# Writing out every engine loop of a decoder step, with all semaphore waits on constants

## The reference

```python
def layer(x, l, mem_k, mem_v, shift_prev, wkv_prev, conv_prev, ffn_prev, v_first, P):
    xn = rmsnorm(x, P['norm_mix'][l])
    proj = xn @ w_in                                   # 1024 -> 3328
    y_a, wkv_new, v_first = rwkv7_group(p_rwkv, p_prev, wkv_prev, v_first, l, P)
    conv_out, conv_new = causal_dwconv(gate_c * h_in, conv_prev, P['conv_w'][l])
    x = x + jnp.concatenate([y_a, gate_b * conv_out], axis=-1) @ P['w_out'][l]
    q = rmsnorm(x, P['norm_x'][l]) @ P['wq'][l]        # 4 heads x 256, 256 memory tokens
    x = x + softmax_attention(q, mem_k, mem_v) @ P['wo'][l]
    up = rmsnorm(x, P['norm_ffn'][l]) @ P['w_up'][l]   # 1024 -> 2 x 2816
    upc, ffn_new = causal_dwconv(up, ffn_prev, P['ffn_conv_w'][l])
    u, gt = jnp.split(upc, 2, axis=-1)
    x = x + (jax.nn.silu(gt) * u) @ P['w_down'][l]
```

## Time and profile before

| | |
|---|---|
| time, median of 3 runs | 4897.39 us |
| the three runs | 4886.02, 4897.39, 4908.73 us |
| span of the profiled execution, first to last instruction | 4900.2 us |
| TensorE busy | 4308.0 us, 88% of the span |
| VectorE, ScalarE, GpSimd busy | 2273.0, 1456.1, 1416.4 us |
| mean granted TensorE clock | 0.914 of full speed |
| moved by DMA | 320.54 MB, 65 GB/s |

### The profile page before, as it was taken

The page is one execution under the profiler, slowest core; times in us unless marked ns, Lnnn a source line. Parts: engine busy times, 40 slices in busy tenths (PEclk is TensorE's granted clock), DMA queues, the critical chain, the costliest instruction groups (busy, mean ns, idle before and its releaser), DMA issues.

```text
span 4900.2 us, 72602 instructions
## 1 busy us (share of the span) xinstructions
PE 4308.0 (88%) x22425; PEld 3583.0 (73%) x22425; DVE 2273.0 (46%) x4969; ACT 1456.1 (30%) x2858; POOL 1416.4 (29%) x1222
## 2 busy tenths in 40 slices
PE   3789988998889989997989889997989787899996
PEld 3569866886679757885779667885879665678885
DVE  1246534545255535454266535444154553245554
ACT  1333233333333233333323233333322212022222
POOL 6232032443231123442331124442221011023331
PEclk9899998998889999998999899997998888699997
DMA  2320122332310112332310213332210112222221
GB/s 73 125 69 1 43 69 65 94 94 73 103 44 1 60 52 86 94 97 77 88 32 0 78 44 103 94 94 78 64 31 0 52 35 86 90 61 73 68 68 57
DMA packets 454929, 320.54 MB, mean 65 GB/s; under 512 B 18012, under 2 KB 420262, under 8 KB 453070
## 3 DMA queue, kind: packets, MB, share of 16 engines
q1 hardware_dynamic: 454758, 318.45, 21.1%
HBM read 296.99 MB, written 21.61 MB: 65 GB/s over the span
## 4 chain that ended last, share of the span: by engine, by line
PE 68%; DVE 15%; issue 9%; POOL 3%; ACT 3%; DMA 1%; DVEq 1%; ACTq 0%; POOLq 0%; SPq 0%
PE psum L671 66%; DVE xlo L1429 2%; PE psum L675 2%; POOL wlo L577 1%; DVE xT L1429 1%; DVE shifted L1429 1%; DVE zr L1432 1%; DVE ws L1429 1%; ACT whi L1102 1%; DVE shifted L1432 1%; DVE kkn_y L1429 1%; POOL stage L519 1%; DVE xT L1432 0%; DMA out_y_prompt<-zr 0%; ACT stage L1102 0%
## 5 line engine op out<-in xcount | busy, mean ns | idle before, releaser
L577 POOL TENSOR_TENSOR wlo<-wraw,whi 128x1024 fp32r<-128x1024 f32 x480 | 1152.3, 2401 | 2818.6 <-ACT whi L1102 2818.5
L671 PE MATMUL psum<-xhi,whi 128*128 128x512 f32 (+1 forms) x3136 | 1254.3, 400 | 58.5 <-DVE xlo L1429 41.1
L671 PE MATMUL psum<-xhi,wlo 128*128 128x512 f32 (+1 forms) x3136 | 1224.0, 390 | 0.0
L671 PE MATMUL psum<-xlo,whi 128*128 128x512 f32 (+1 forms) x3136 | 1224.0, 390 | 0.0
L1102 ACT ACTIVATE whi<-wraw 128x1024 fp32r<-128x1024 f32 x480 | 507.4, 1057 | 1226.2 <-PE psum L671 1161.4
L671 PEld LDWEIGHTS psum<-xhi,whi 128*128 128x128 f32 x3136 | 599.7, 191 | 231.6 <-DVE xlo L1429 81.1
L671 PEld LDWEIGHTS psum<-xhi,wlo 128*128 128x128 f32 x3136 | 599.7, 191 | 125.0
L671 PEld LDWEIGHTS psum<-xlo,whi 128*128 128x128 f32 x3136 | 601.2, 192 | 113.0 <-issue 1.4
L1429 DVE TENSOR_TENSOR xT<-xT,psum 128x512 f32<-128x512 f32 (+1 forms) x416 | 286.0, 688 | 246.0 <-PE psum L671 166.5
L1741 DVE TENSOR_SCALAR zr<-zr,fcw 128x512 f32<-128x512 f32 x176 | 91.9, 522 | 585.2 <-POOL fcarry L619 583.5
L671 PE MATMUL psum<-ws 128*128 128x64 f32 (+1 forms) x2560 | 350.7, 283 | 2.1 <-DVE ws L1595 1.7
(11 more groups left out here) (292 smaller groups left out, 5587.7 us busy)
## 6 DMA issues: line engine op xcount, KB each, us to landing
wraw<-in_w_up SPq DMA_DIRECT2D x176, 512.0 KB, 3.8
wraw<-in_w_in SPq DMA_DIRECT2D x104, 512.0 KB, 3.9
wraw<-in_w_down SPq DMA_DIRECT2D x88, 512.0 KB, 3.5
wraw<-in_w_out SPq DMA_DIRECT2D x32, 512.0 KB, 4.1
wraw<-in_wq SPq DMA_DIRECT2D x32, 512.0 KB, 4.0
wraw<-in_wo SPq DMA_DIRECT2D x32, 512.0 KB, 4.1
kkn_y<-in_x_prompt SPq DMA_DIRECT2D x4, 2048.0 KB, 9.3
xT_scratch<-xT SPq DMA_DIRECT2D x4, 2048.0 KB, 7.6
```

What stands on the lines that cost most here:

```text
L577: return e.tensor_tensor(wlo[i][:, :, :], wraw[i][:, :, :], whi[i][:, :, :].bitcast(F32), ALU.subtract).then_inc(lo_ready[i], 1)
L671: return e.matmul(out, lhsT, rhs, start=start, stop=stop)
```

## The change

All hardware loops become loops of the program that writes the instructions, so each turn's instructions stand in the stream one after the other. Turn numbers are then constants, and so is every wait's value and every address. The register operations, the branches and the three `passed` semaphores go. The order of the work on data, the buffers and the other semaphores stay. The diff, cut to its core; the same edit is made at each loop and at each count of `passed`:

```diff
 class Counts:
-    def __init__(self, eng, name, passed=None):
-        self.eng, self.name, self.passed, self.n, self.turns = eng, name, passed, {}, []
+    def __init__(self):
+        self.n = {}

     def __call__(self, sem, k=1):

         v = self.n[sem.name] = self.n.get(sem.name, 0) + k
-        for i, per in self.turns:
-            if per.get(sem.name):
-                v = i * per[sem.name] + v
         return v
...
-    @contextmanager
-    def loop(self, label, count):
-        key = f"{self.name}.{label}"
-        per, before = LOOPS.get(key, {}), dict(self.n)
-        if self.passed is not None and self.turns:
-            self.eng.sem_inc(self.passed, 1)
-        with self.eng.Fori(0, count) as i:
...
             def carries(a, tile):
                 e.wait_ge(eb_ready[a], c(eb_ready[a]))
-                e.sem_inc(passedG, 1)
...
-                with c.loop("ffn", NF // 2 - 1) as i:
+                for i in range(NF // 2 - 1):
                     ffn_up(i + 1)
                     ffn_down(i)
...
-            with c.loop("block", NB - 1) as b:
+            for b in range(NB - 1):
                 one_block(b, False)
             one_block(NB - 1, True)
```

More of the change, by code:

```diff
@@ L580, in splits @@
             def splits(label, pairs):
-                with c.loop(label, pairs):
+                for _ in range(pairs):
                     split(0)
@@ L937, in one_block @@
                 head_rows(8)
-                with c.loop("gates" + "s" * last, 4):
+                for _ in range(4):
                     dense(0, 0, s)
@@ L944, in one_block @@
                 wkv_pair(True)
-                with c.loop("wkv", NC // 2 - 1):
+                for _ in range(NC // 2 - 1):
                     wkv_pair()
@@ L986, in one_block @@
                 ffn_up(s, tuple(range(KT)))
-                with c.loop("ffn" + "s" * last, NF // 2 - 1):
+                for _ in range(NF // 2 - 1):
                     ffn_up(s)
@@ L1138, in _ @@
                 split_x(k, NMEM)
[L1139 removed]
+            for _ in range(8):
                 for j in range(2):
@@ L1352, in one_block @@
                 ffn_hidden()
-                with c.loop("ffn" + "s" * last, NF // 2 - 1) as i:
+                for i in range(NF // 2 - 1):
                     ffn_up(i + 1)
@@ L1644, in residual @@
                 acc_start()
-                with c.loop(label + "s" * last, KT // 2) as i:
+                for i in range(KT // 2):
                     for j in range(2):
@@ L1884, in one_block @@
                 e.wait_ge(a2v, c(a2v, 4))
-                with c.loop("h_in" + "s" * last, 2) as i:
+                for i in range(2):
                     for j in range(2):
```

158 lines of the change are left out of this document (22 added, 136 removed).

## The result

| | before | after |
|---|---|---|
| median of four runs | 4900.91 us | 4784.85 us |
| lowest and highest | 4886.02, 4908.73 us | 4781.53, 4790.23 us |

The ratio is 0.9764, with a 95% interval of 0.9744 to 0.9783. Six more runs of the changed kernel, with another set of runs of before, gave 4781.80 us and 0.9739 (0.9713 to 0.9764).

The account below looks back on a forecast made before the run. TensorE, busy 88% of the time, was taken as the bound, with register operations costing where short dependent chains reach it late. Terms of 8.9 + 10.5 + 8 + 6.4 + 7.5 + 0.5 = 42 us gave 4855 us, range 4812 to 4890.

Parts of the forecast that it names:

- A: Back-edges of the block loop: both crossings that branch back become as short as the one falling through, 8.9 us.
- the carry-to-silu chain: Convolution chain in `ffn` of blocks 0 to 2: from 2.90 us to the constant form's 2.55 us.
- C: `ffn` turns of the last block: two TensorE gaps per turn that end on VectorE's sequencer shrink, 8 us.
- the supply of instructions: Rival, slower by fetching straight code: some 270 packets, up to 5118 us if each fully blocked TensorE; chance 0.08.
- B: `ffn` turns of blocks 0 to 2: 0.35 us of register operations saved in each of 30 turns, 10.5 us.
- the cap of 0.39: Most that a shorter chain could give at an `ffn` turn's edge: 0.39 us per turn, 11.8 us in all.
- the fall-through: Crossing into the last block without branching back, 32.81 us, taken as the form of all three crossings after the change.
- D: `wkv` pairs: removing both levels of turn numbers gains 6.4 us; upper bound 19 us, all of TensorE's idle time.
- the nearest row: `wkv` pair with one level of turn numbers less: 51.44 to 51.26 us, 0.18 us, taken twice for the second level.
- The counts of `passed`: Extra semaphore counts on which nobody waits: their removal was put at nothing.
- E: Norms, attention and projections' edges: 2.5 us a block, 7.5 us for blocks 0 to 2; bounds 0 and 49 us.
- The clock: Low-clock stretch in one last-block `wkv` pair, 22.8 us: 23 us either way, in the range but not the sum.

Follow-up runs that it names:

- dve_wkv_kept: Changed kernel, but VectorE's loop over chunk pairs in `wkv` stays a hardware loop with one level of turn numbers: 4825.23 us.
- dve_clean: Kernel before, with all loops written out on VectorE alone and VectorE's extra counts taken out too: 4821.03 us.
- passed_kept: Changed kernel, straight code with constant waits, but the extra counts of `passed` stay behind their waits: 4806.98 us.
- dve_only: Kernel before, with all loops written out on VectorE alone and the extra counts left in: 4813.20 us.
- blk_only: Kernel before, with only the block loop written out, on all engines; shorter loops stay hardware loops: 4857.03 us.
- gap_d: Changed kernel with 18 small fills in each `wkv` pair on VectorE, behind waits for TensorE, without register operations: 4810.00 us.
- late_a: Changed kernel with 40 small fills of an unused tile on VectorE ahead of the first block: 4790.73 us.

## Why the prediction was wrong

**What held.** The signs and places of the parts that it named; the 5.6 us ahead of block 0 were in none. TensorE was the bound, A's back-edges went, the carry-to-silu chain fell to 2.55 us, the gaps of C closed, and the supply of instructions cost nothing: packets rose to 179 (270 were estimated), while TensorE ran 2320 matmuls in 426.05 us without a break. In B the eight middle turns of a block gave 0.44 us each, 10.4 us in all. That is above the cap of 0.39, whose pace of 0.229 us had counted in the length of the turn's last matmul. The other 7.5 us of B lie in the first turn and after the ninth, at the edges of the stage, which the sum had left out. A was 3 us short, since the fall-through, its model, got faster as well (32.81 to 32.17 us) and the other two fell below it.

**The step that failed first: D.** The prediction took "the nearest row", 0.18 us for one level of turn numbers, and doubled it for the other level. The levels are not alike: a middle pair takes 51.45 us with two, 51.17 with one (dve_wkv_kept), 49.99 with none. The second level costs 0.28 us; the first costs 1.2 us, together with the loop's end and VectorE's counts, which go with it. The upper bound, TensorE's idle time in the pair (1.6 us, 19 us in all), was the better estimate: 18.3 us were had. That is partly luck, since half of the idle time is left and TensorE's busy time fell instead.

**The edit costed at nothing: the counts.** "The counts of `passed`, on which nobody waits" looked at who waits for them, not at where they stand. Each is an instruction of its own between a wait and the data behind it. Left in, they cost 22 us in the finished kernel, of which the profile books 9 us directly and the rest in attention's clock. Whose counts are the costly ones is open: taking VectorE's out beside engines with loops (dve_clean) brought 0.1 us a pair.

**E was sampled at two stages and bounded by the wrong row.** Without attention E gave 19.3 us, inside the bounds of 0 to 49, instead of 7.5. The upper bound came from DVEq's 1%, where the issue latencies beside the register operations are larger than these. And the last block, taken as the form after the change, moved as well: its head-norm stretch fell from 24.56 to 22.69 us. The register pieces of VectorE's chain in it are the same before and after. What got shorter is TensorE's work, 64 small matmuls from 6.59 to 5.35 us among it, at a granted clock of 0.77 instead of 0.72. Their rows before and after:

```profile
3876.57 6.59 PE L671 MATMUL psum<-ident,sm 128*64 128x128 f32 x64 [0.93 <-DVEq L1946]
3767.83 5.35 PE L552 MATMUL psum<-ident,sm 128*64 128x128 f32 x64 [0.93 <-DVEq L1816]
```

The granted clock of block 1's `out` stage, which fell from 53.43 to 50.78 us, also went from 0.96 to 0.99. So E holds a part that is clock, for which it had no term; how large it is, no run separates.

**The clock was left out of the sum.** It is the largest part of the 78 us that the sum lacked: 22.8 us of the stretch and 12.1 us of attention. The stretch was seen, and the prediction said that the change "may move such a pair in or out". It moved out, in all ten runs of the changed kernel. Of the kernels with VectorE's `wkv` waits in registers, six of seven have runs 20 to 72 us apart, those of before in steps of some 20 (4882, 4903, 4923, 4950); the eleven kernels without have 50 runs, and no kernel's runs within one set are more than 10 us apart. Before's median lies some 20 us above its lowest run; that is what the change gained there. That it hangs on VectorE's register work in `wkv` is shown by dve_wkv_kept, one loop and its counts away from the changed kernel (passed_kept, with the counts and without the loop, has no stretch), and by dve_only's even runs. blk_only is the exception: it has that loop in registers, and neither a stretch in its profile nor runs more than 4 us apart. So that work does not always bring a stretch, and by which property it does is open, after gap_d. The 12 us of attention moved with small delays, with no edit in attention; that they hang on where the stage falls in time fits all profiles but is not shown further.

By the Trainium skill (Runtime: NRT & Kernel Launch, section Instruction fetch mechanics), straight code is fetched ahead and a far branch must wait. Both sides agree here: the 179 packets under gapless matmuls, and the crossings. The crossing out of block 1 goes from 37.25 to 32.87 us when the block loop alone is written out on all engines (blk_only), to 33.8 us with VectorE alone (dve_clean), stays at 37.3 us with TensorE alone, and reaches 31.66 us in the changed kernel.

By the rule on the pipeline's flush (the Trainium skill, VectorE: DVE Perf Modes, section The DRAIN you can't avoid) B should have been 0. It was not: a register operation between two dependent instructions is not covered by the flush here, as the carry-to-silu chain shows, 2.90 us before and 2.55 after.

## What to carry to other kernels

Price a register operation or a separate semaphore count by the gap between the two data instructions around it, on the chain that ends in the bounding engine; the page's share for the sequencer misses the latency beside it. In this kernel the first level of loop indices, with the loop's end and the counts that came with it, cost 1.2 of 1.45 us a pair, so a copy of the code with one level less was no model of constants. Where a stage leaves the bounding engine only a small idle time and the chain into it is full of such operations, weigh that idle time as an estimate beside the nearest small difference; here it was much the closer. And where a profile shows one stretch at the lower clock among equal ones, compare several runs: steps of one size between them suggest that the stretch is a cost in the median, which an edit may remove.

## What was not expected of the hardware

TensorE's granted clock in the same attention matmuls lay between 0.77 and 0.88, and its time between 53.0 and 60.4 us, in 19 profiles; in late_a, with a delay of 2.4 us well ahead of it, it was another. Stretches of 47.8 us at 1.2 GHz, at a cost of some 23 us each, came in `wkv`, with TensorE busy for nearly the whole pair before and after. And writing out ScalarE, GpSimd and SyncE alone made the kernel slower than before (1.0042, 1.0014 to 1.0070), with pairs 0.4 us longer and runs up to 72 us apart, though its profiled execution had a span 24.5 us shorter than that of before. That execution is its fastest run and has no stretch at the lower clock; so the slower median is, as far as the steps between the runs tell, one stretch more.
